# The beginning of a two-layer diffusion step: half chunks, small parts, four more load places and a new order of requests

## The reference, cut to what matters

```python
m = jax.nn.silu(cond) @ w_mod + b_mod                 # six vectors: sm, cm, gm, sf, cf, gf
h = rms_norm(x, norm_mix_pre[l]) * (1 + cm) + sm
z = h @ w_in[l]                                       # 2048 x 4608, split into q, k, v, u, v_c
```

## Time and profile before

| | |
|---|---|
| median of three runs | 2321.32 us (2320.76 to 2325.68) |
| the profiled execution | 2317.93 us, its span 2316.2 us, mean granted clock 0.996 |
| PE busy | 2247.0 us (97%) |
| DVE, ACT, POOL busy | 1622.3, 984.9, 66.5 us |
| read from HBM | 603.79 MB, 263 GB/s over the span |
| first product of the projection | at 38.19 us |

### The profile page before, as it was taken

One profiled execution on the slowest core, in us unless ns is written; L12 is line 12 of the kernel. 1 busy time (PEld: TensorE's weight loads), 2 busy tenths in 40 slices (PEclk: granted clock), 3 DMA queues, 4 the chain that ended last, 5 costly groups with the idle time before them and its releaser, 6 DMA issues.

```text
span 2316.2 us, 27842 instructions
## 1 busy us (share of the span) xinstructions
PE 2247.0 (97%) x10614; PEld 1778.0 (77%) x10614; DVE 1622.3 (70%) x1734; ACT 984.9 (43%) x1277; POOL 66.5 (3%) x97
## 2 busy tenths in 40 slices
PE   5999989999999999999999999999999999999998
PEld 3766666678888888888877886787888888888886
DVE  3555473488988989889887996557888544554555
ACT  3333253464444444334446344346444444434443
POOL 1000120000000000000000101000000000000000
PEclk9999999999999999999999999999999999999999
DMA  9899989868878878888866998766887666666664
GB/s 364 323 334 341 337 317 330 300 220 289 282 271 292 289 265 283 295 279 290 307 209 225 312 315 283 271 204 207 270 263 263 185 196 185 190 189 193 191 225 146
DMA packets 269365, 609.91 MB, mean 263 GB/s; under 512 B 19100, under 2 KB 19280, under 8 KB 267824
## 3 DMA queue, kind: packets, MB, share of 16 engines
q1 hardware_dynamic: 264832, 589.37, 75.4%
q0 software_dynamic: 4400, 18.75, 2.3%
HBM read 603.79 MB, written 5.45 MB: 263 GB/s over the span
## 4 chain that ended last, share of the span: by engine, by line
PE 87%; DVE 4%; DMA 4%; ACT 3%; issue 1%; POOL 1%; SPq 1%; POOLq 0%; DVEq 0%; ACTq 0%
PE bank_A L961 41%; PE bank_B L961 39%; DMA mraw<-in_mod_w 3%; PE bank_X L1049 2%; PE bank_M L1025 2%; DVE wlo L1564 1%; PE bank_M L1009 1%; ACT junk L1285 1%; ACT whi L1271 1%; DMA x<-in_x_sample 0%; DVE x L1674 0%; ACT prob L1436 0%; PE bank_M L950 0%; DVE xt_lo L1615 0%; PE bank_T L1042 0%
## 5 line engine op out<-in xcount | busy, mean ns | idle before, releaser
L1564 DVE TENSOR_TENSOR wlo<-raw,whi 128x1024 fp32r<-128x1024 f32 x724 | 880.6, 1223 | 587.3 <-ACT whi L1271 586.4
L1271 ACT CAST whi<-raw 128x1024 fp32r<-128x1024 f32 x724 | 759.5, 1051 | 1162.6 <-PE bank_A L961 575.5
L961 PE MATMUL bank_B<-whi,xt_lo 128*128 128x512 f32 x1104 | 433.3, 392 | 0.0
L961 PE MATMUL bank_A<-whi,xt_lo 128*128 128x512 f32 x1088 | 428.9, 394 | 3.7 <-DVE xt_lo L1615 3.7
L961 PE MATMUL bank_B<-wlo,xt_hi 128*128 128x512 f32 x1104 | 430.0, 389 | 0.0
L961 PE MATMUL bank_B<-whi,xt_hi 128*128 128x512 f32 x1104 | 429.8, 389 | 0.0
L961 PE MATMUL bank_A<-wlo,xt_hi 128*128 128x512 f32 x1088 | 425.0, 391 | 0.0
L961 PE MATMUL bank_A<-whi,xt_hi 128*128 128x512 f32 x1088 | 424.7, 390 | 0.0
L1585 DVE SCALAR_TENSOR_TENSOR acc<-mraw,cond,acc 128x1024 f32<-128x1024 f32 x300 | 371.2, 1279 | 0.0
L961 PEld LDWEIGHTS bank_A<-whi,xt_lo 128*128 128x128 f32 x1088 | 205.0, 188 | 65.1 <-issue 23.2
L961 PEld LDWEIGHTS bank_B<-whi,xt_lo 128*128 128x128 f32 x1104 | 207.2, 188 | 53.8 <-issue 11.7
(11 more groups left out here) (242 smaller groups left out, 1567.7 us busy)
## 6 DMA issues: line engine op xcount, KB each, us to landing
mraw<-in_mod_w SPq DMA_DIRECT2D x352, 512.0 KB, 6.0
raw<-in_w_gate SPq DMA_DIRECT2D x176, 512.0 KB, 4.4
raw<-in_w_up SPq DMA_DIRECT2D x176, 512.0 KB, 4.4
raw<-in_w_down SPq DMA_DIRECT2D x176, 512.0 KB, 5.0
raw<-in_w_in SPq DMA_DIRECT2D x144, 512.0 KB, 5.4
raw<-in_w_out SPq DMA_DIRECT2D x64, 512.0 KB, 5.8
z<-in_mod_w SPq DMA_DIRECT2D x12, 512.0 KB, 11.5
spare<-in_mod_w SPq DMA_DIRECT2D x8, 512.0 KB, 9.5
```

Source lines behind the costliest of these rows:

```text
L961: mm = pe.matmul(bank[f"{pair}{s}"][:], xs[:, k, t], w[:, kb, :], start=(k == first and n == 0), stop=(k == (nk - 1 if last is None else l ...
L1271: act.copy(weights(u * UNIT + ph)[0], raw[:, ph % RING]).then_inc(hi_ready, 1)
L1564: dve.tensor_tensor(lo, raw[:, ph % RING], hi.bitcast(F32), ALU.subtract).then_inc(lo_ready, 1)
```

## The change

**Halves.** The chunks 0 and 1 are loaded and multiplied in two column halves (`HALVED` = 2): four loads of 512 rows x 256 columns (rows of 1 KB in HBM), four products each (`halved_piece`). The first halves (the modulation of row blocks 0 and 1 of the quarter) are done ahead of the first product, the second halves behind the pieces 2 and 5.

**Parts.** `PARTS` has row blocks 0 and 1, 2 and 3, then 4 to 7, 8 to 11, 12 to 15. In the first 18 pieces each visit is one piece: nine column chunks for the first part, nine for the second. DVE so reads a pair after each of them. Scaling is in steps 6 and 15, then as before in step 13 of a quarter. `pre_part` scales and casts two row blocks. Two warming products (`keep_warm`) stand ahead of piece 0.

**Places.** `OWN` are the first 12 loads and 16 to 19. Of the later bursts of the first projection every second one (`idle_turn`) goes to four more places (`qkt` twice, `hid`, `sil`), so that room is freed by the load eight before.

**Requests.** SP asks for x first, then half of chunk 0, a w_in piece, half of chunk 1, then w_in pieces with the rest between them. POOL's constants are in another order, with three semaphores (`c_loaded`, `const_loaded`, `table_loaded`); `vrows` is turned in two steps (banks X0 and X1). The bursts of the first quarter are moved to 8, 10, 12, 14, and one more is in the last. `ATT_PIECE` goes from 62 to 65.

```diff
-START_BURSTS = [QUARTER * n + r for n, rs in enumerate(((1, 4, 7, 10, 14), (1, 4, 7, 10, 13, 16), (1, 4, 7, 10, 13, 16), (1, 4, 7, 13)))
+START_HALVES = {2: 0, 5: 1}
+START_BURSTS = [QUARTER * n + r for n, rs in enumerate(((8, 10, 12, 14), (1, 4, 7, 10, 13, 16), (1, 4, 7, 10, 13, 16), (1, 4, 7, 9, 13)))
                 for r in rs]
-START_FETCH = {g + 3 + h: (m, js[2 * h:2 * h + 2]) for g, (m, js) in START_MOD.items() if m > 2 for h in range(2)}
+START_FETCH = {1: (0, range(4, 6)), 2: (0, range(6, 8)), 3: (1, range(4, 5)), 4: (1, range(5, 6)), 5: (1, range(6, 7)), 6: (1, range(7, 8))}
+for i, g in enumerate(START_BURSTS):
+    first = (7, 9, 11, 14)[i] if i < 4 else START_BURSTS[i - 2] + 6
+    START_FETCH.update({first + h: (START_MOD[g][0], START_MOD[g][1][2 * h:2 * h + 2]) for h in range(2)})
...
+START_TURNS = {QUARTER * n + 12: n + 1 for n in range(ND - 1)}
+START_SCALES = {6: 1, 15: 2, QUARTER + 13: 3, 2 * QUARTER + 13: 4}
+ATT_PIECE = QUARTER * 3 + 11
...
+PARTS = [range(0, 2), range(2, 4), range(4, 8), range(8, 12), range(12, 16)]
 def start_piece(q):
     n, r = divmod(q, QUARTER)
-    return n, r // 2, 2 * n + r % 2
+    return (r // W_INC, r % W_INC, r // W_INC) if n == 0 else (n + 1, r // 2, 2 * n + r % 2)
+def visit_begins(q):
+    return q < QUARTER or q % 2 == 0
...
+OWN = [*range(0, 12), *range(16, 20)]
+START_END = 16 + 4 * 21
+def idle_turn(q):
+    i = (q - 16) // 4
+    return i // 2 if q < START_END and i > 0 and i % 2 else None
 def ring_before(q):
-    n = ring_turn(q) - RING
-    return n if n < RING else n + (2 * UNIT - RING) if n < 2 * RING else n + 2 * UNIT
+    return q - 12 if q < 28 else q - 8 if q < START_END else q - RING
...
# SP
-            for m in range(2):
-                mod_chunk(m, 0, range(UNIT), start_chunk(m))
-                for q in range(1, LEAD) if m else range(1):
-                    start_load(q)
-            mod_chunk(2, 0, range(UNIT), start_chunk(2))
-            for q in range(LEAD, ND * QUARTER):
+            for s in range(2):
+                sp.dma_start(x[:, s, :], xin[s]).then_inc(x_loaded, 16)
+            mod_chunk(0, 0, range(0, 4), start_chunk(0))
+            start_load(0)
+            mod_chunk(1, 0, range(0, 4), start_chunk(1))
+            for q in range(1, ND * QUARTER):
                 start_load(q)
                 if q in START_FETCH:
...
# TensorE, start()
+                mod(0, range(0, 4))
+                start_tail(0)
+                mod(1, range(0, 4))
                 turn_x(0, 0, 0)
                 turn_x(0, 0, 1)
+                start_tail(1)
+                free("A0", use["A0"])
+                keep_warm("A0", 2)
...
-                    if r % 2 == 0:
+                    if visit_begins(q):
                         for s in range(2):
                             free(f"{pair}{s}", use[f"{pair}{s}"] + e // 2)
-                    if r == 0:
-                        pe.wait_ge(xt_ready, 2 * (n + 1))
+                    pe.wait_ge(xt_ready, 2 * (p + 1))
                     pe.wait_ge(lo_ready, q + 1)
...
+            def halved_piece(m, j):
+                q = ring_piece(m, j)
+                w = mod_place(q) if q in OWN else mraw[:, q % RING].rearrange("p t (h n) -> p (t h) n", n=CH // 2)
+                for t in range(4):
+                    k = 4 * (j % 4) + t
+                    mm = pe.matmul(bank["M"][32 * t:32 * t + 32, 0:CH // 2], cond[:, 2 * k:2 * k + 32], w[:, t, :],
+                                   start=(k < 4), stop=(k >= KD - 4))
...
# VectorE, start()
                 for q in range(1, LEAD):
                     split(0, q)
                 normal(0, 0, 4, 5, 6, 7)
                 for q in range(ND * QUARTER):
...
                     split(0, q + LEAD)
-                    if r % 2:
-                        read_part(n, c, q)
-                    if q - 3 in START_ENDS:
-                        m = START_ENDS[q - 3]
-                        mod_cols(m, start_chunk(m))
-                    if n + 1 < ND and r == 13:
-                        part(n + 1)
+                    if visit_ends(q):
+                        read_part(p, c, q)
+                    if q - 1 in START_ENDS:
+                        start_cols(START_ENDS[q - 1])
+                    if q in START_SCALES:
+                        part(START_SCALES[q])
```

More of the change, by code:

```diff
@@ L152, in ring_piece @@
 def ring_piece(m=None, j=0, v=None, i=0):
+    if v is None and m < HALVED:
+        return UNIT * (j // 4) + 4 * m + j % 4
     if v is None:
@@ new lines, with tail_chunk @@
+START_ENDS = {g: mod_tail_of(m) for g, (m, js) in START_MOD.items() if js[0] and (m < MOD_INIT or m == MOD_INIT + ND - 1)}
+START_MOD.update({g: (m, range(4, 8)) for g, m in START_HALVES.items()})
+START_ENDS.update({g: HALVED + m for g, m in START_HALVES.items()})
+START_TURNS = {QUARTER * n + 12: n + 1 for n in range(ND - 1)}
+START_SCALES = {6: 1, 15: 2, QUARTER + 13: 3, 2 * QUARTER + 13: 4}
+ATT_PIECE = QUARTER * 3 + 11
+def tail_chunk(i):
+    return (start_chunk(i % HALVED), slice(2 * (i // HALVED), 2 * (i // HALVED) + 2)) if i < 2 * HALVED else (start_chunk(i - HALVED), slice(0, 4))
@@ L272, in __init__ @@
         self.take("X0")
+        self.take("X1")
         self.mods(MOD_INIT)
@@ L612, in vec_count @@
         def vec_count(l, which):
-            return 2 * l + which + ND
-        N_CONST = 12
+            return 2 * l + which + len(PARTS)
+        N_C = 4
+        N_CONST = 6
+        N_TABLE = 2
         N_ATT = 12
@@ L790, in _ @@
                 load(vrows[0:96, 1 + l, :], a["mod_b"][l].rearrange("(t p) -> t p", p=P), const_loaded)
[L791 to L798, removed]
+            load(rope[:], a["c_rope"].rearrange("p (a b) -> p a b", a=2), table_loaded)
+            load(edge[:], a["c_edge"], table_loaded)
             def power(src, dst, s_in, n_in, s_out):
@@ L1040, in vector_turn @@
                 free("T", i)
-                for t in range(4):
+                for t in range(2 if i < 2 * HALVED else 4):
                     mm = pe.transpose(bank["T"][:, t * P:(t + 1) * P], mrow[:, t * P:(t + 1) * P], ident[:])
@@ L1168, in attention @@
                 return got
+            pe.wait_ge(c_loaded, 16 * N_C)
+            free("X0", 0)
+            pe.transpose(bank["X0"][:, 3 * P:4 * P], vrows[:, 3, :], ident[:]).then_inc(filled["X0"], 1)
             pe.wait_ge(const_loaded, 16 * N_CONST)
[L1172 to L1175, removed]
+            free("X1", 0)
+            for t in range(3):
+                mm = pe.transpose(bank["X1"][:, t * P:(t + 1) * P], vrows[:, t, :], ident[:])
+            mm.then_inc(filled["X1"], 1)
             pe.wait_ge(cond_ready, 1)
@@ L1299, in row, with start_row, pre_part @@
                     act.wait_ge(filled["T"], i)
-                act.copy(mrow[:], bank["M"][:]).then_inc(mrow_ready, 1)
+                c = slice(0, CH // 2 if i < 2 * HALVED else CH)
+                act.copy(mrow[:, c], bank["M"][:, c]).then_inc(mrow_ready, 1)
+            def start_row(i):
+                act.wait_ge(mod_used, 4 * (i + 1) if i < 2 * HALVED else
+                            (i - HALVED) * UNIT + UNIT if i - HALVED < MOD_INIT else (MOD_INIT + ND) * UNIT)
+                row(i)
+            def pre_part(p):
+                fill_of(*plan.at[(0, "pre_uses", 0)][1])
+                bk, n = plan.at[(0, "pre_uses", 0)][1]
+                for k in PARTS[p]:
+                    ins = act.activation(xtmp[:, 0, 1, k, :], bank[bk][:, k * P:(k + 1) * P], ACT.Identity,
+                                         scale=scal[:, k, 1:2], bias=shift[:, k, 1:2])
+                ins.then_inc(freed[bk] if p else part_scaled[1], 1)
+                for s in range(2):
+                    bk, n = plan.at[(0, "pre_uses", 0)][s]
+                    if p:
+                        act.wait_ge(freed[bk], n + 2)
+                    else:
+                        act.wait_ge(part_scaled[s], 1)
+                    ks = slice(PARTS[p][0], PARTS[p][-1] + 1)
+                    high(xt_hi[:, ks, s * P:(s + 1) * P], xtmp[:, 0, s, ks])
             def pre_scale(l, which, i):
@@ L1726, in start, with part @@
             def start():
-                def part(n):
-                    norm_vectors(0, 0, slice(4 * n, 4 * n + 4), 2 * (n + 1))
-                    dve.wait_ge(vec_ready, n + 1)
-                    pre_pair(0, 0, 2 * n)
-                mod_cols(0, start_chunk(0))
+                def part(p):
+                    ks = slice(PARTS[p][0], PARTS[p][-1] + 1)
+                    norm_vectors(0, 0, ks, 2 * (p + 1))
+                    dve.wait_ge(vec_ready, p + 1)
+                    if p > 1:
+                        return pre_pair(0, 0, 2 * (p - 1))
+                    bk, n = plan.at[(0, "pre_uses", 0)][0]
+                    fill_of(bk, n)
+                    for k in PARTS[p]:
+                        ins = dve.tensor_scalar(xtmp[:, 0, 0, k, :], bank[bk][:, k * P:(k + 1) * P], scal[:, k, 0:1],
```

(10 more changed lines are left out.)

170 lines of the change are left out of this document (97 added, 73 removed).

## The result

Over 17 executions of each, the changed kernel took 2325.57 us (median; 2323.24 to 2330.13), the one before 2321.93 (2318.01 to 2325.68, and one stray execution of 8042.92, which does not enter the ratio). The ratio is **1.0021, 95% interval 1.0014 to 1.0028**: slower by 0.2%, 3.3 to 6.5 us; the medians are 3.6 apart. The forecast was 1.3 us slower, 2322.5, with a range of 2311 to 2329.

The account below looks back on a forecast made before the run. The prediction took PE, busy 97% of the span, as the bound, behind a load-limited beginning. Its terms, +3.1 + 2.1 - 5.8 + 0.9 + 1.0, gave +1.3 us, 2322.5 us; range 2311 to 2329.

Parts of the forecast that it names:

- Step 1: At the beginning: reordered, partly half-width loads bring PE's first product to 26, 12 us earlier.
- half clock: Behind the stop before the third visit: PE's slow clock costs 1.7 us, as behind the first product before.
- Step 2: Before the third visit: PE waits for a bank read until 37.9; the 12 us head start shrinks to 5.4 plus 0.3.
- Half bursts: Two in the first 18 pieces, each 1.25 us with its refill, between 1.0 and 2.1.
- Step 3: Visits of one piece in the first 18: PE waits for bank reads, 0.6 us before 5 and 0.6 before 8.
- Step 4: The two scalings, in pieces 6 and 15: 0.9 us lost before visit 9 and 3.9 before visit 18.
- Step 5: SP's queue: w_in 15 and 16 come late because SP waits for the burst after piece 10; visit 14 loses 1.5 us.
- Step 6: From piece 18 on: four more places remove 4.2 us of modulation-load waits and 1.6 of slow clock, 5.8 earlier.
- Step 7: Seam: a slow-clock stretch from the stop before piece 18 costs 0.9 us, w_out loads at the projection's end 1.0.
- (b): Rival, first 18 pieces: three more clock falls cost 5.1 us, the seam's upper end 1: 2328.6; chance 0.14.
- (a): Rival, third visit: head start kept, idle under 1 us, 7.8 less: 2314.8, or 2311 with scaling partly hidden; chance 0.27.
- (c): Rival, later bursts: the four places bring nothing, loads late by bandwidth, 4 of the 5.8 us stay: 2326.5; chance 0.13.

Follow-up runs that it names:

- read first: Changed kernel with DVE reading a visit's banks before splitting the piece four ahead, in the first 18 pieces: 2312.99 us, ratio 0.9959 to the kernel before.
- loads first: Changed kernel with SP asking for w_in 1, 2 and 3 ahead of the second halves of chunks 0 and 1: 2323.68 us, ratio 1.0000.
- places alone: Kernel before, with only the four more places and their earlier requests added, its beginning untouched: 2316.66 us, ratio 0.9972.
- w_out first: Changed kernel with the first four w_out pieces ahead of the four modulation loads that wait for the burst after 67: 2323.35 us, ratio 1.0006.
- the run without places: Changed kernel without the four more places, a burst's loads mistakenly asked for three positions earlier than before the change: 2427.93 us, ratio 1.0444.
- all three: Changed kernel with banks read before the split in the first 18 pieces, w_in 1 to 3 earlier, and w_out ahead of modulation loads: 2309.28 us, 0.9948.
- both orders: Changed kernel with banks read before the split in the first 18 pieces and w_in 1 to 3 ahead of the second halves: 2312.57 us, 0.9963.
- the places of the first quarter only: Changed kernel with the four more places only in its first quarter, later loads going through the ring of four: 2337.92 us, ratio 1.0072.

## Why the prediction was right, and by how much it was off

The direction and the mechanism were right: the head start is real and the stops eat it. The sum said +1.3, the medians +3.6, the interval of the ratio 3.3 to 6.5. Of the signs named, the first product (27.95 for 26), the idle of about 5 before the third visit (4.62), the one of about 4 before piece 18 (3.56) and the missing waits for mraw after 110 came; the products ended at 298.1 and not near 296. By its steps:

- **Step 1.** Forecast 26, the first product was at 27.95. The loads landed as worked out (the last products began at 21.53 for 21.2); those products, the x turns and the row's transposes, at half clock from 20.4 to 27.2, took most of the rest. It cost nothing, as step 2 said: the third visit doesn't depend on it.
- **Step 2.** Forecast a stop to 37.9, measured 38.30, ended by a DVE read, with half clock behind. The half clock lasted 6.8 us and not 3.4; piece 2 lost 2.7 for the 1.7 forecast, and the half burst 0.3. The last link was one that the sum had not priced: DVE had done its normalising at 34.65 and then waited 1.12 for the cast of piece 4, whose w_in load landed at 34.7. The load of piece 3 landed 0.5 earlier than forecast, so the end came out nearly right by some luck. The "33" for the end of pieces 0 and 1 doesn't follow from 26 and two pieces (31.4), but enters no sum. That one order of DVE and one of SP each shorten the stop is shown (read first, loads first).
- **Half bursts, a term that was mis-sized.** I took 1.25 each. They took 2.14 (in part at half clock) and 1.86, and 0.27 of refill. The trace counts 32 products in one where a whole burst has 16 of twice the width. It is the same work: 16 row blocks of 256 columns against 8 of 512, which the diff says and I overlooked. At full clock the miss is two times 0.9, 1.8 us.
- **Step 3.** Forecast 0.6 before 5 and 0.6 before 8: measured 0.73 and 0.73.
- **Step 4.** Forecast 0.9 before piece 9 and 3.9 before 18: 0.61 and 3.56.
- **Step 5.** Forecast 1.5 before piece 14: 2.19, and behind it a stretch of half clock that I had not counted, 1.9. The chain has the w_in load that waited for SP.
- Together piece 18 started at 110.8 and not at 104.4. Of these 6.4, 3.2 are half clock, the term that was mis-sized most (forecast 1.7, measured 3.0 behind piece 2's stop and 1.9 behind 14's), 1.8 the half bursts, 0.7 the stop before 14, the rest small terms.
- **Step 6.** Forecast 5.8 earlier. From piece 18 to piece 68 the kernel before took 182.3 us, the changed one 176.2 with one burst (2.1) more: 8.2 earlier. The places alone gave 0.9972, 6.5 us, with the longer stop at the seam in it.
- **Step 7.** The half clock did not come behind the stop before 18 but behind the one at the seam, and lasted 6.8. The seam's stop was 4.41 instead of 2.07, 2.3 more, above the upper end of 2; from piece 68 to the fifth piece of w_out the changed kernel falls back by 3.0 more, and w_out first took 3.5 us off. So the seam costs 3.0 to 3.5 and not 1.9.

The errors were +6.4 in the first quarter, -2.4 in the places and +1.1 at the seam (3.0 for 1.9): +5.1, so that a sum by the measured terms is 6.4 late, which is what the trace shows behind the attention. The median of the runs is only 3.6 above the one before, and the granted clocks say why in part: the profiled execution of the changed kernel, at 0.991, is 4.6 above its own median, the one of the kernel before, at 0.996, is 4.0 below its own, and at the same clock the kernels are some 3 us apart. Where the half clock fell in the other executions isn't recorded. That the forecast came within 3.1 us of the median is thus partly luck: two errors cancelled in part, and the profile from which the terms are measured has more half clock than most executions.

Of the rivals, (b) was half right: in the profile the clock made half of the miss in the first quarter (3.2 of 6.4) and part of the seam's, in stretches behind stops of 4.6, 2.2 and 4.4; its time of 2328.6 was not reached by the median. (a) failed on the step it named (the stop was 4.6, not under 1), and (c) is refuted by the run with the places alone. The Trainium skill (TensorE: Matmul & The Clock Gate, A second HAM failure mode) says that frequent short idles in a cycle through the PSUM banks can make the clock go down and up. For the short stops that is not borne out in this trace: behind those of 0.5 to 0.7 the clock stayed up.

## What to carry to other kernels

An engine that starts 12 us earlier gains only what its supply can follow: before moving the start, follow the second and third use of each buffer, and the order in which the engine that frees it works. Where a visit to a bank becomes shorter than the path that frees it, put the freeing instruction ahead of the preparing one; here that one order was worth 0.6% (changed kernel to read first), and nothing that could be told from noise where visits were two pieces long. On a queue that works in order, more places allow earlier requests, and a request that is too early for its place costs far more than one too late: some 100 us in the run without places, against 4.2 of waits in the kernel before.

## What the runs showed of the hardware

- The length of a stop alone does not tell whether half clock comes with it. The stop of 1.8 before piece 18 had none in two kernels (read first, all three) and 3.4 us of it in another (both orders, 96.4 to 99.8, granted 0.50). The stop of 3.56 before piece 18 is the same in four profiles: none in the changed kernel, 3.4 us in w_out first (from 111.0) and in the places of the first quarter only (from 108.7), 6.8 us in loads first (from 102.9). Behind the stop of 2.2 before piece 14 it came in the changed kernel and not in the one with the places in the first quarter only. A stretch of 6.8 at half clock takes at most 3.4 of work from PE (an estimate: half of it), so the price of such a stop is to be given as 0 to 3.4 us beside its own length.
- Rows of 1 KB in the loads cost little. In the trace of the changed kernel a DMA packet of 1 KB took 46 ns and one of 2 KB 84 ns (medians), so the same bytes take 9.5% longer in 1 KB rows; on the 1.3 us that a load of 0.5 MB has of the stream that is 0.12 us, an estimate from these packets, and the prediction took 0.13. With it the last of the first eight half-width loads let PE start its products at 21.53, where the sum had 21.2.
